# Scans stage of a two-block layer kernel: 77 gate products taken out of the steps of the triangular inverses, 81 put in elsewhere, and one RWKV pair product one step later

## The reference, cut to what matters

```python
    proj = h @ w_in
    gates = jnp.split(jax.nn.sigmoid(merge), N_MIXERS, axis=-1)     # merge: the last 4 x 1024 columns of proj
    mixed = gates[0] * (ys[0] @ w_branch[0])
    for i in range(1, N_MIXERS):
        mixed = mixed + gates[i] * (ys[i] @ w_branch[i])
```

## The kernel before

| steps | what |
|---|---|
| 2, 4, 8, 10 | spatial gating: means (2, 4), sums of squares (8, 10) |
| 23 to 47 odd, 91 to 115, 159 to 183, 227 to 251 | inverse of DeltaNet, units 1 to 4 |
| 62 to 86 even, 134 to 158, 206 to 230, 278 to 302 | inverse of RWKV, units 1 to 4 |
| 81 and 85, 149 and 153, 217 and 221 | DeltaNet pair products ("a"; "c") of units 2, 3, 4 |
| 52, 54, 56; 122, 124, 126; 194, 196, 198; 266, 268, 270 | RWKV `first`: bonus product, pair products, rest of the pair products; units 1 to 4 |

## Time and profile before

### The profile page before, as it was taken

One profiled execution on the slowest core, in us unless ns is written; L12 is line 12 of the kernel. 1 busy time (PEld: TensorE's weight loads), 2 busy tenths in 40 slices (PEclk: granted clock), 3 DMA queues, 4 the chain that ended last, 5 costly groups with the idle time before them and its releaser, 6 DMA issues.

```text
span 4078.9 us, 51857 instructions
## 1 busy us (share of the span) xinstructions
PE 3830.4 (94%) x20718; PEld 3011.2 (74%) x20718; DVE 2658.7 (65%) x3054; ACT 1344.8 (33%) x1764; POOL 1193.2 (29%) x578
## 2 busy tenths in 40 slices
PE   8999999999889998999999989999999989999998
PEld 7567788877666766778887767887677767776777
DVE  7964878789865553487878888533545554546783
ACT  5242432244433333242324343212222131324512
POOL 2012044445213332114444422223122221212064
PEclk9999999999889999999999989999989989899999
DMA  3002232354311010223326332223211221323053
GB/s 112 21 26 84 106 108 93 110 181 149 121 68 37 32 37 26 93 98 116 101 92 209 129 133 101 94 104 117 83 56 54 74 78 63 116 75 106 28 205 145
DMA packets 131770, 385.58 MB, mean 95 GB/s; under 512 B 13565, under 2 KB 14209, under 8 KB 126281
## 3 DMA queue, kind: packets, MB, share of 16 engines
q1 hardware_dynamic: 131528, 382.27, 26.8%
HBM read 281.00 MB, written 101.22 MB: 94 GB/s over the span
## 4 chain that ended last, share of the span: by engine, by line
PE 71%; DVE 22%; ACT 3%; issue 2%; POOL 1%; DMA 1%; DVEq 0%; SPq 0%; ACTq 0%; POOLq 0%
PE ps L380 22%; PE ps L1453 21%; PE ps L476 8%; PE ps L2976 3%; PE ps L4489 2%; PE ps L907 2%; PE ps L2250 1%; DVE acc L1722 1%; PE ps L2242 1%; DVE top L1626 1%; DVE xop L1626 1%; PE ps L3077 1%; DVE x L661 1%; PE ps L4153 1%; DVE t L641 1%
## 5 line engine op out<-in xcount | busy, mean ns | idle before, releaser
L333 POOL TENSOR_TENSOR wlo<-wraw,whi 128x1024 fp32r<-128x1024 f32 x181 | 446.9, 2469 | 1772.4 <-ACT whi L325 1763.8
L1453 PE MATMUL ps<-xop,whi 128*128 128x512 f32 x1984 | 618.1, 393 | 14.3 <-DVE acc L1747 9.6
L325 ACT ACTIVATE whi<-wraw 128x1024 fp32r<-128x1024 f32 x185 | 196.1, 1060 | 921.3 <-PE ps L380 610.9
L1453 PE MATMUL ps<-top,whi 128*128 128x512 f32 x1488 | 468.3, 396 | 19.7 <-DVE acc L1716 15.9
L1453 PEld LDWEIGHTS ps<-xop,whi 128*128 128x128 f32 x1984 | 373.0, 188 | 99.3 <-DVE acc L1747 12.1
L1453 PE MATMUL ps<-xop,wlo 128*128 128x512 f32 x992 | 388.1, 391 | 0.0
L476 PE MATMUL ps<-xhalf,whi 128*128 128x512 f32 x1024 | 374.0, 448 | 0.3 <-POOL wlo L333 0.3
L1453 PEld LDWEIGHTS ps<-top,whi 128*128 128x128 f32 x1488 | 280.6, 189 | 87.6 <-DVE acc L1716 19.0
L1851 POOL TENSOR_TENSOR wlo<-wsum,whi 128x1024 fp32r<-128x1024 f32 (+2 forms) x102 | 229.1, 2246 | 362.7 <-ACT whi L1478 362.4
L380 PE MATMUL ps<-xhi,whi 128*128 128x512 f32 x868 | 307.0, 435 | 20.7 <-DVE xlo L681 9.1
L1453 PE MATMUL ps<-top,wlo 128*128 128x512 f32 x744 | 293.5, 394 | 0.0
(11 more groups left out here) (637 smaller groups left out, 7132.8 us busy)
## 6 DMA issues: line engine op xcount, KB each, us to landing
wraw<-in_w_dram SPq DMA_DIRECT2D x185, 512.0 KB, 3.5
h_keep<-h SPq DMA_DIRECT2D x154, 256.0 KB, 4.5
wraw<-in_s_dram SPq DMA_DIRECT2D x48, 512.0 KB, 4.1
f<-h_keep SPq DMA_DIRECT2D x24, 768.0 KB, 5.5
wmore<-in_s_dram SPq DMA_DIRECT2D x32, 512.0 KB, 4.0
x_keep<-x SPq DMA_DIRECT2D x16, 1024.0 KB, 3.8
g_keep<-gates SPq DMA_DIRECT2D x64, 256.0 KB, 2.4
gb<-g_keep SPq DMA_DIRECT2D x32, 512.0 KB, 3.7
```

The source lines that it names most:

```text
L325: se.own().activation(K.hi(c), K.raw[:, c % NRAW, :], ACT.Copy).then_inc(*K.S(("hi", c)))
L333: ge.own().tensor_tensor(K.lo(c), K.raw[:, c % NRAW, :], K.hi(c).bitcast(F32), SUB).then_inc(*K.G(("lo", c)))
L1453: d = pe.e.matmul(out[:, s, :], w[:, o], x[:, i, :], start=(j < 3 and i == 0 and t == 0), stop=(i == k - 1 and t == 2), skip_group_check=True)
```

## The change

`MORE_GATES` gets new values, and one `yield` in the `first` of RWKV moves up by one line, so that the third pair product goes from the step of the first two into the next step, where the fourth is.

In numbers (after minus before, for each of the 337 steps): 77 steps have one gate product fewer. Each of them is a step of an inverse (x or t products), nine or ten for each of the eight inverses. 33 steps have more, 81 in all: 2 and 4 (one each), 8 (3), 22 (1), 23 (2), 42 (4), 47 (3), 52 (1), 56 (4), 75, 81, 85 (2 each), 91, 115 (1 each), 122, 124 (3 each), 143 (2), 153, 159 (3 each), 181 (1), 189, 191 (2 each), 193 (4), 194 (5), 195 (1), 196 (3), 202 (4), 211 (1), 217, 221, 256 (3 each), 266 (5), 268 (2). The stage has 450 gate products instead of 446 (512 in all, so 62 instead of 66 go beside the attention). Before, an inverse has 1 gate product behind each x step and mostly 2 behind each t step; after, it has 0 and 1. One more stands behind the other stream's step in between, in both versions.

In SP's table the entry 4 is overwritten in both versions, so the new product at step 4 is missing there: from then on SP is one gate step behind the other engines' count, where it was level before.

```diff
--- before.py
+++ after.py
@@ -3556,8 +3556,8 @@
         yield
         pairs_tensor(pe, K, Q, ((n, 0), "a"), part(0, 64), B.BE, B.AL, (n, "al"), (n, "be"))
         pairs_tensor(pe, K, Q, ((n, 0), "b"), part(0, 64), B.KA, B.AL, (n, "ka"))
+        yield
         pairs_tensor(pe, K, Q, ((n, 1), "a"), part(1, 64), B.BE, B.AL)
-        yield
         pairs_tensor(pe, K, Q, ((n, 1), "b"), part(1, 64), B.KA, B.AL)
         turn_tensor(pe, K, Q, (n, "a0"), B.V, (n, "a0 in"))
         yield
@@ -4308,7 +4308,7 @@
-MORE_GATES = {1: 12, 18: 3, 27: 1, 31: 1, 35: 1, 39: 1, 43: 3, 47: 5, 66: 1, 70: 1, 74: 1, 78: 1, 82: 1, 88: 2, 95: 1, 99: 1, 103: 1, 107: 1, 111: 5, 115: 5, 138: 1, 142: 1, 146: 1, 150: 1, 154: 1, 158: 2, 163: 1, 167: 1, 171: 1, 175: 1, 179: 4, 181: 3, 210: 1, 214: 1, 218: 1, 222: 1, 226: 7, 228: 8, 231: 1, 235: 1, 239: 1, 243: 1, 247: 1, 251: 7, 282: 1, 286: 1, 290: 1, 294: 1, 298: 1, 303: 2, 313: 6}
+MORE_GATES = {1: 12, 2: 1, 4: 1, 8: 3, 18: 3, 22: 1, 23: 2, 25: -1, 29: -1, 31: 1, 33: -1, 37: -1, 41: -1, 42: 4, 43: 2, 47: 8, 52: 1, 56: 4, 64: -1, 68: -1, 72: -1, 75: 2, 76: -1, 80: -1, 81: 2, 85: 2, 88: 2, 91: 1, 93: -1, 97: -1, 101: -1, 105: -1, 109: -1, 111: 5, 115: 6, 122: 3, 124: 3, 136: -1, 140: -1, 143: 2, 144: -1, 148: -1, 152: -1, 153: 3, 158: 2, 159: 3, 161: -1, 165: -1, 169: -1, 173: -1, 177: -1, 179: 4, 181: 4, 189: 2, 191: 2, 193: 4, 194: 5, 195: 1, 196: 3, 202: 4, 208: -1, 211: 1, 212: -1, 216: -1, 217: 3, 220: -1, 221: 3, 224: -1, 226: 6, 228: 8, 229: -1, 233: -1, 237: -1, 241: -1, 245: -1, 251: 7, 256: 3, 266: 5, 268: 2, 280: -1, 284: -1, 288: -1, 292: -1, 296: -1, 303: 2, 313: 6}
```

## The result

The changed kernel takes 4086.1 us (median of 6 runs, 4083.0 to 4088.6), the kernel before 4072.3 beside it (6 runs, 4069.2 to 4073.4): ratio 1.0029, 95% interval 1.0017 to 1.0041. It is slower by 13.8 us, where 16 us less were forecast. The profiled execution of the change has a span of 4081.7 us (4083.5 with what lies around it); that of before, 4080.7, was 7.6 us above its median, so the two traces differ by less than the medians.

What follows compares the result with a forecast made beforehand. TensorE, busy 94% of the span, was taken as the bound, losing time to waits and half clock. Waits net -5 and clock -11 made -16 us, taking the median from 4073.15 to 4057, range 4034 to 4080.

Steps and rivals of the forecast that it cites:

- (b): RWKV unit 2, steps 122 to 126: added products cover most of 4.8 us of waits, 2.1 left, -2.7 us.
- (c): RWKV unit 3, steps 189 to 198: 17 added products cut waits of 8.9 us to 3.5, -5.4 us.
- (d): RWKV units 4 and 1: unit 4's pair wait falls by 1.9 us, its bonus wait stays; unit 1 gains 0.7.
- (a): Spatial gating at step 8, -1.4 us, and DeltaNet's first turn at step 23, -0.7 us, from products ahead.
- (e): Tiles' scaling and tanh move away from two ScalarE waits in the inverses: -2 us of 3.7, bounds 0 and -3.7.
- the first sum: Total of the waits expected to shrink in the scans stage: -14.8 us.
- Waits that grow: The inverses' own waits (+5.0 us) and DeltaNet's pair products at 81, 217 and behind L3250: +9.8 us in sum.
- the subtraction: Time to spare at each of 77 thinned inverse steps: 14 have under 0.68 us, costing 0.05 to 0.67 each, 5.0 together.
- The clock: Half-clock stretches after RWKV's pair products mostly go (-11 us), behind staying waits -3, elsewhere +3: net -11 us.
- Rival 2: Thinned inverses no longer keep the clock up; it falls once in each of eight: +27, net +11, 4084 us; chance 0.12.
- Rival 1: Added products stand behind the waits, so few gain and the clock falls at the same places: 4070 us; chance 0.22.
- Rival 3: Every half-clock stretch behind a wait ends earlier: clock -26, waits -10, 4037 us; chance 0.16.

Runs made afterwards that it cites:

- e5_tiles: Changed kernel with three gate products moved so a tile's scaling and tanh stand behind ScalarE's copies at steps 23 and 143: 4077.2 us, 1.0002 to before.
- e14_cut_after: Changed kernel with GpSimd's weight split done on 128 of 1024 columns, part of the computation left out: 4057.1 us, 0.9941 to before.
- e8_thin_rw: Kernel before with 39 gate products taken from RWKV's four inverses only and put at thick steps right behind them: 4103.3 us, 1.0066 to before.
- e9_thin_dn: Kernel before with 37 gate products taken from DeltaNet's four inverses only and put at thick steps behind them: 4068.2 us, 0.9986 to before.
- e7_units: Kernel before plus moved pair product, with products from DeltaNet's inverses (37) and steps 226, 228 (8) put at waits of RWKV's units: 4045.3 us, 0.9928.
- e2_table: Kernel before with the change's new table alone, the pair product left where it was: 4087.1 us, 1.0030 to before.
- e3_loads: Changed kernel with the loads' table at step 4 raised from 12 to 13: 4087.8 us, 1.0025 to before.
- e1_yield: Kernel before with the moved pair product alone, gate products where they were: 4073.6 us, 0.9998 to before.
- e12_attend: Changed kernel with four products fewer at step 313, so the attention has the 66 of before: 4085.5 us, 1.0019 to before.
- e6_ahead: Changed kernel with 18 gate products at DeltaNet's waiting steps put two steps earlier: 4074.2 us, 0.9995 to before.
- e11_more: e7_units with 16 more products moved from thick steps 115, 179, 181 and 251 to steps where it still waits: 4041.1 us, 0.9902 to before.
- e13_cut_before: Kernel before with GpSimd's weight split done on 128 of 1024 columns, part of the computation left out: 4046.0 us, 0.9918 to before.

## Why the prediction was wrong, point by point

- **Waits that shrink, (b) and (c).** Right for L3692. Unit 2 forecast -2.7, measured 5.3 to 2.8, in part by luck: what is left stands at the bonus product (2.77), not at L3646, and 2 us of it are the stretched L3682; with the split cut 0.9 and 0.6 are left. Unit 3, steps 189 to 198, forecast -5.4, measured 10.0 to 4.0, and step 202 lost 1.9 more. "No wait above 2 us for L3692" held, and the half clock after unit 2's pair products shrank from 10.1 us to 3.4 (3111.8 to 3115.2).
- **(d).** Unit 1 gave 4.3, not 0.7: three waits lay in reach of its products. Unit 4 gave nothing: 2.52 at the bonus and 1.86 at the pair became 0.46, 3.05 for L3646 and 0.98. Here the wait for L3692 only became one for L3646, as the prediction named for its own failing.
- **(a) and (e), the failed step of the first sum.** Step 8 lost its 1.8 and step 22 its 0.55, but 1.39 came at step 16. For the tiles I took -2 with bounds of 0 and -3.7, as if the move could only help; "others will be hit instead" stood there without a price. Steps 23 and 143 took 4.2 and 3.8 us more. The tile's place did most of it (e5_tiles took 2.8 and 3.2 back), but about 2 us of each need the split as well: they go in e14_cut_after, with the tile where it was. Of the two waits of 3.7 that were to go, one fell from 1.96 to 0.83 and one from 1.65 to 1.15; that one is put down to issue in its row, not to ScalarE. The bounds should have been symmetric.
- **Waits that grow, forecast +9.8, the step that failed most.** It asked of each of the 77 removed products whether the inverse's own chain had 0.68 us to spare, and added one or two products at each of the waits of DeltaNet that it named. In the four stretches of RWKV's inverses alone the waits grew by 19.3. What had a term came near it: the inverses' own waits at L2976 grew by 6.5 against 5.0, those at 81, at 217 and behind L3250 by 6.1 against 4.8. What had none made the rest: 3.8 at 143, 3.4 at 149, 2.2 at steps 68, 73, 137 and 141. What was missed is that the stretch is the cover of DeltaNet's back and pair chain over its whole length, not one product ahead of each wait: ten products taken out and four put in between steps 64 and 85 are 4 us of cover less, and the waits there grew by 3.4. With the split cut the growth is the cover lost to within 1.2 us in each of the three stretches. In the kernel as it is, the place of a tile (143) and the collisions come on top: 149 went from none to 3.38 with L3232 stretched to 2.75 beside the split, and with the cut it is 1.5; 85 went from 0.96 to 2.98, and with the cut it is 1.05, while 81 takes the loss. Of the growth 4.7 us are RWKV's own inverse (226, 286, 288), which the subtraction had as small waits of 0.05 to 0.67. e8_thin_rw shows the loss by itself. e9_thin_dn shows that the subtraction was good for DeltaNet's inverses, but for 1.6 us at step 31, where 0.7 was the most named; that RWKV has no such chain beside them is read from the order of the steps, not shown by a run.
- **The clock, forecast -11, measured about 0** (325 us at half, not 326). In e7_units, where nothing takes it back, the gain is -26. In the change it was paid back beside RWKV's inverses (50 to 86 us, 18 us of time), where the +3 for "waits that grow at 81 and 217" stood: six times too small. 21 of these 36 us are in the fourth stretch, which went from 1.00 to 0.85; e2_table, with the same waits in it, has 4 us at half clock there, so its size is one trace's.
- **Attention, loads, weights, the move's order.** As predicted, nothing for the loads and the move's order (e3_loads, e1_yield); for the attention nothing that can be told (e12_attend). At unit 3, gate products waited 1.4 us in sum for the inputs' renewal, L2779, within the bounds given.
- **The rivals.** Rival 2 gave the right time, 4084, and the right term, but its mechanism, a fall in each thinned inverse, is refuted as I put it: DeltaNet's second to fourth inverse, thinned, ran at 1.00 (the rows of e9_thin_dn), and in three of RWKV's it is mostly longer waits of the other stream beside which the clock falls. RWKV's fourth is the exception: there the thinned inverse itself waits 1.12 and 2.17 and the clock falls, the prediction's own sign of being wrong. Rival 1 is true for step 85 (e6_ahead). Rival 3 is what e7_units shows, once the products come from the right place. The section on a second failure mode of the clock gate in the Trainium skill, "TensorE: Matmul & The Clock Gate", which I weighed for rival 2, is not borne out by a row here either: the waits beside which the clock falls are few and long.

What stays open: why executions of one kernel differ so much in granted clock (93 of the kernel before had 0.955 to 0.965, 80 us of half-clock time apart); why e5_tiles and e6_ahead, with 11 us more of waits than the kernel before, are no slower; and how much of the gains of e5_tiles, e6_ahead and e7_units beyond their waits is due to which stretch. One trace of each does not tell. No run gives the changed kernel back the products of RWKV's inverses alone; e7_units, which comes nearest, differs from it elsewhere too.

## What to carry to other kernels

Filler work is not spare where its own neighbours can do without it: before moving it, sum the cover that the other streams lose from the start of their chain to its end, and take only from stretches beside which no chain runs (here, with the products put elsewhere too, that turned +14 us into -32). If a count of fillers also sets where evictions and conversions fall, price that as a cost of either sign. And do not price a wait by its length alone, since the clock goes with it, if loosely: 16 us more of waits cost 26 in e8_thin_rw and 15 more cost 14 in the change, 10 less were worth 32 in e7_units, and 9 less again only 4 in e11_more.

## What the runs showed of the hardware

VectorE operations without an operand in PSUM that begin during a GpSimd operation of 2.4 us last up to 2.8 us instead of 0.7; those with one are not stretched (none of 103 in the changed kernel). In this stage that costs up to 31 us of 4077 (e13_cut_before). I had not expected the size, nor that halving the GpSimd operation would not help: 26 stretched operations instead of 17, 22 us of excess instead of 26, and no time that can be told.
